# A hybrid decoder step on one core: the conv history, the last conv taps and y cross HBM with channels on the partitions

## What is computed

```python
def conv_ffn(h, hist, w_up, conv_w, conv_b, w_down):
    T = h.shape[1]
    g_pre, u = jnp.split(h @ w_up, 2, axis=-1)
    gp = jnp.concatenate([hist.astype(g_pre.dtype), g_pre], axis=1)
    conv = conv_b + conv_w[0] * gp[:, 0:T]
    for i in range(1, CONV_W):
        conv = conv + conv_w[i] * gp[:, i:i + T]
    y = (jax.nn.silu(conv) * u) @ w_down
    return y, gp[:, T:]
...
    x = x + gate2 * y
```

## Time and profile before

| | |
|---|---|
| median of 3 runs | 1593.41 us (1593.29 to 1593.66) |
| profiled execution, span from first to last instruction | 1592.4 us |
| PE busy | 1569.0 us (99%), 12242 matmuls |
| DVE, ACT, POOL busy | 899.9, 665.7, 74.4 us |
| mean granted TensorE clock | 0.995 |
| DMA | 371.06 MB, mean 233 GB/s |

### The profile page before, as it was taken

One profiled execution on the slowest core, in us unless ns is written; L12 is line 12 of the kernel. 1 busy time (PEld: TensorE's weight loads), 2 busy tenths in 40 slices (PEclk: granted clock), 3 DMA queues, 4 the chain that ended last, 5 costly groups with the idle time before them and its releaser, 6 DMA issues.

```text
span 1592.4 us, 29203 instructions
## 1 busy us (share of the span) xinstructions
PE 1569.0 (99%) x12242; PEld 1418.5 (89%) x12242; DVE 899.9 (57%) x1525; ACT 665.7 (42%) x935; POOL 74.4 (5%) x131
## 2 busy tenths in 40 slices
PE   8999999999999999999999999999999999999997
PEld 4777888888888658888899999999999999999997
DVE  3555776656667536447454545545454566656663
ACT  3433444434446335325333333333333445545552
POOL 2000000001111000000000000000000000000000
PEclk8999999999999999999999999999999999999999
DMA  9999877777778998988844444454545554555460
GB/s 338 387 366 329 303 263 265 254 269 242 243 261 297 390 398 300 330 321 302 284 159 161 161 161 160 160 185 142 181 164 171 166 162 147 191 157 191 146 192 20
DMA packets 239232, 371.06 MB, mean 233 GB/s; under 512 B 7793, under 2 KB 188371, under 8 KB 230905
## 3 DMA queue, kind: packets, MB, share of 16 engines
q1 hardware_dynamic: 231888, 351.19, 63.8%
q0 software_dynamic: 7152, 17.90, 3.4%
q10 hardware_dynamic: 66, 0.14, 0.0%
HBM read 359.32 MB, written 9.88 MB: 232 GB/s over the span
## 4 chain that ended last, share of the span: by engine, by line
PE 84%; DMA 5%; issue 5%; DVE 3%; SPq 2%; ACT 2%; POOL 0%; ACTq 0%; POOLq 0%; DVEq 0%
PE ps L1046 24%; PE ps L1047 23%; PE ps L1048 23%; PE ps L998 3%; PE ps L1289 2%; DMA ring<-in_w_in 2%; PE ps L991 1%; DMA proj<-in_cache_v_win 1%; DMA vals<-in_w_ada 1%; SPq L610 1%; DMA ring<-in_w_out 1%; DVE wlo L2173 1%; PE ps L1360 1%; PE ps L1329 1%; ACT whi L1608 1%
## 5 line engine op out<-in xcount | busy, mean ns | idle before, releaser
L1046 PE MATMUL ps<-hhi,whi 128*128 128x288 f32 x3120 | 929.7, 298 | 1.5 <-DVE wlo L2014 0.5
L1047 PE MATMUL ps<-hlo,whi 128*128 128x288 f32 x3120 | 917.1, 294 | 0.0
L1048 PE MATMUL ps<-hhi,wlo 128*128 128x288 f32 x3120 | 917.0, 294 | 0.0
L1046 PEld LDWEIGHTS ps<-hhi,whi 128*128 128x128 f32 x3120 | 585.3, 188 | 43.6 <-issue 33.9
L1047 PEld LDWEIGHTS ps<-hlo,whi 128*128 128x128 f32 x3120 | 585.6, 188 | 0.7
L1048 PEld LDWEIGHTS ps<-hhi,wlo 128*128 128x128 f32 x3120 | 585.4, 188 | 0.0
L2014 DVE TENSOR_TENSOR wlo<-ring,whi 128x1024 fp32r<-128x1024 f32 x178 | 212.2, 1222 | 89.2 <-ACT whi L1599 88.8
L1599 ACT ACTIVATE whi<-ring 128x1024 fp32r<-128x1024 f32 x178 | 184.2, 1056 | 155.0 <-PE ps L1048 148.4
L2173 DVE TENSOR_TENSOR wlo<-ring,whi 128x1024 fp32r<-128x1024 f32 x96 | 117.0, 1222 | 84.6 <-ACT whi L1608 84.4
L1608 ACT ACTIVATE whi<-ring 128x1024 fp32r<-128x1024 f32 x96 | 100.8, 1053 | 145.6 <-PE ps L1048 112.3
L2695 DVE TENSOR_TENSOR wlo<-ring,whi 128x1024 fp32r<-128x1024 f32 (+1 forms) x94 | 105.7, 1132 | 56.0 <-ACT whi L1935 56.0
(11 more groups left out here) (323 smaller groups left out, 1141.5 us busy)
## 6 DMA issues: line engine op xcount, KB each, us to landing
ring<-in_w_up SPq DMA_DIRECT2D x88, 1024.0 KB, 5.2
ring<-in_w_ada SPq DMA_DIRECT2D x64, 1024.0 KB, 7.6
ring<-in_w_in SPq DMA_DIRECT2D x48, 1024.0 KB, 8.1
ring<-in_w_down SPq DMA_DIRECT2D x32, 1408.0 KB, 6.7
proj<-in_w_ada SPq DMA_DIRECT2D x28, 1024.0 KB, 9.4
ring<-in_w_out SPq DMA_DIRECT2D x16, 1024.0 KB, 8.6
ring<-in_cache_k_win SPq DMA_DIRECT2D x12, 1024.0 KB, 8.5
proj<-in_cache_v_win SPq DMA_DIRECT2D x8, 1024.0 KB, 13.1
```

The costliest lines, as they stand in the source:

```text
L1046: mm(out, w_hi, x_hi, start=start, stop=False)
L1047: mm(out, w_hi, x_lo, start=False, stop=False)
L1048: return mm(out, w_lo, x_hi, start=False, stop=stop)
```

## The change

The host lays `state_conv` out as [partition, tile, 16 rows] ahead of the launch, and takes `new_conv` and `y` as [partition, tile, rows]; it rearranges them after. In the kernel:

- the whole history comes in one load of 128 x 704 elements into `tail`, at the point of the first load of before; DVE copies from it to `gpad`;
- DVE writes the last taps of all 44 tiles to `last_taps` (in `gates`), stored by one DMA behind the last turn;
- `yst` is stored as it is, two tiles at a time, by POOL;
- all turns of up and down on PE are gone, with ACT's and DVE's copies out of the banks, and the waits between them;
- the last chunk of down goes tile 2 first, then tile 3; DVE finishes tile 2 and tile 3 apart; ACT stores tile 2, SP stores tile 3;
- SP, not POOL, waits for the output DMAs.

```diff
@@ up and down, PE
-                pe.wait_ge(hist_in[par], i * 8 + (16 - 8 * par))
-                pe.wait_ge(*FV.upto("hist", i - 1))
-                pe.sem_inc(row_turns, 1)
-                for n in range(4):
-                    last = turn(ps[:, 4, 16 * n:16 * n + 16], hrow[:, par, P * n:P * n + P], ident[0:16, 0:16])
-                last.then_inc(*FT.step("hist"))
...
-                pe.wait_ge(*FV.upto("last", i))
-                pe.wait_ge(*FA.upto("rows", i - 1))
-                for n in range(4):
-                    last = turn(ps[0:18, 5, P * n:P * n + P], glast[:, n, :], ident)
-                last.then_inc(*FT.step("rows"))
...
-                            for k in range(nk):
-                                for n in range(2):
...
+                            end = i == 3 and j == 23
+                            order = [(k, n) for k in range(nk) for n in range(2)]
+                            for k, n in sorted(order, key=lambda kn: kn[1]) if end else order:
...
+                                if end and (k, n) == (nk - 1, 0):
+                                    last.then_inc(last_even_done, 1)
                             last.then_inc(used, 1)
-                            if i == 3 and j == 22:
-                                first_row_turns()
-                        if i and kg == 0 and h == 0:
...
-                            row_turns_of(i - 1)
-            row_turns_of(3)
@@ POOL
+            pool.dma_start(history.rearrange("p n b r -> p (n b r)"), a["state_conv"].rearrange("p n c -> p (n c)")
+                           ).then_inc(hist_in, 16)
+            pool.wait_ge(*FV.upto("last", 10))
+            pool.dma_start(o["new_conv"], last_taps).then_inc(conv_out, 16)
+            for i in range(4):
+                for h in range(2 if i < 3 else 1):
+                    pool.wait_ge(*DV_.upto(f"u{h}", i))
+                    pool.dma_start(o["y"][:, 4 * i + 2 * h:4 * i + 2 * h + 2], yst[:, 2 * h:2 * h + 2]
+                                   ).then_inc(y_out[h], 16)
@@ ACT
-                act.wait_ge(*FT.upto("rows", i))
-                act.wait_ge(conv_stored, i + 1)
-                f(crows, ps[0:18, 5, :], ACT.Copy).then_inc(*FA.step("rows"))
...
+            act.wait_ge(*DV_.upto("u1", 3))
+            act.dma_start(o["y"][:, 14], yst[:, 2]).then_inc(last_even_out, 16)
@@ DVE
-                dve.wait_ge(*FT.upto("hist", i))
+                dve.wait_ge(hist_in, 16)
                 v.tensor_copy(gpad[:, :, 2 + SEQ:GW].rearrange("p n (b t) -> p n b t", t=6)[:, :, :, 0:2],
-                              ps[:, 4, 0:64].rearrange("p (n b r) -> p n b r", n=4, b=NB)).then_inc(*FV.step("hist"))
+                              history[:, 4 * i:4 * i + 4]).then_inc(*FV.step("hist"))
...
-                    dve.wait_ge(*DT.upto("t2", i - 1))
+                    if i:
+                        dve.wait_ge(y_out[h], 16 * i)
...
+                def last_out():
+                    dve.wait_ge(y_out[1], 48)
+                    dve.wait_ge(last_even_done, 1)
+                    dve.wait_ge(*DV_.upto("u0", 3))
+                    gated(5 * KD, 14, ps[:, 2:3, :], lambda m: yst[:, 2, :], DV_, 1, 3)
+                    dve.wait_ge(used, 3 * 24 + (CH_DOWN + BUFS + 24))
+                    dve.wait_ge(*DV_.upto("u1", 3))
+                    gated(5 * KD, 15, ps[:, 3:4, :], lambda m: yst[:, 3, :], DE, 0, 0)
@@ SP
-            sp.wait_ge(first_row_out, 1)
-            sp.dma_start(o["y_p"][0:P, 1536:2048], yrow[0]).then_inc(y_end_out, 16)
+            sp.wait_ge(*DE.upto("u", 0))
+            sp.dma_start(o["y"][:, 15], yst[:, 3]).then_inc(last_odd_out, 16)
+            for s, n in ((conv_out, 16), (k_out, 256), (v_out, 256), (stp_out, 64), (s0_out, 128), (y_out[0], 64),
+                         (y_out[1], 48), (last_even_out, 16), (last_odd_out, 16)):
+                sp.wait_ge(s, n)
```

More of the change, by code:

```diff
@@ L903, in _ @@
[L903 to L915, removed]
@@ L1479, in up_turn @@
                     unit(2, 2 * n + 1, i * 16 + CH_UP, last_slabs(i, 2 * n + 1))
-                pe.wait_ge(*FV.upto("last", i))
-                pe.wait_ge(*FA.upto("rows", i - 1))
-                for n in range(4):
-                    last = turn(ps[0:18, 5, P * n:P * n + P], glast[:, n, :], ident)
-                last.then_inc(*FT.step("rows"))
-            for i in range(11):
[L1487 to L1511, removed]
+            for i in range(11):
+                up_turn(i)
             pe.wait_ge(*FA.upto("g1", 10))
@@ L2544, in _, with gated @@
             head_lo(1)
-            def gated(gate, tile, psum, out, steps, n, i, end=False):
-                tmp = tmp_s[:, 64 * (n % 2):64 * (n % 2) + 64]
-                ts = tmp.rearrange("p (n b t) -> p n b t", n=2, b=NB)
-                gs = modT[:, bass.ds(tile + gate, 2), 1:NC9].rearrange("p n (b a) -> p n b a", a=1)
+            def gated(gate, tile, psum, out, steps, n, i):
+                c = psum.shape[1]
+                tmp = tmp_s[:, 64 * (n % 2):64 * (n % 2) + NS * c]
+                ts = tmp.rearrange("p (n b t) -> p n b t", n=c, b=NB)
+                gs = modT[:, bass.ds(tile + gate, c), 1:NC9].rearrange("p n (b a) -> p n b a", a=1)
+                first, last_step = (f"s{n}", f"u{n}") if steps is not DE else ("s", "u")
                 v.tensor_tensor(ts, psum[:, :, SEQ:TOK].rearrange("p n (b t) -> p n b t", t=TS),
-                                gs.to_broadcast([P, 2, NB, TS]), ALU.mult).then_inc(*steps.step(f"s{n}"))
-                for m in range(2):
-                    last = v.scalar_tensor_tensor(
+                                gs.to_broadcast([P, c, NB, TS]), ALU.mult).then_inc(*steps.step(first))
+                for m in range(c):
+                    v.scalar_tensor_tensor(
                         out=out(m)[:, 0:SEQ], in0=psum[:, m, 0:SEQ],
@@ L2558, in gated @@
                         op0=ALU.mult, op1=ALU.add)
-                if end:
-                    last.then_inc(last_shown, 1)
-                dve.wait_ge(*steps.upto(f"s{n}", i))
-                for m in range(2):
+                dve.wait_ge(*steps.upto(first, i))
+                for m in range(c):
                     last = v.tensor_tensor(out(m)[:, SEQ:TOK], tmp[:, NS * m:NS * m + NS],
                                            xT[:, bass.ds(tile + m, 1), SEQ:TOK].rearrange("p a c -> p (a c)"), ALU.add)
-                last.then_inc(*steps.step(f"u{n}"))
+                last.then_inc(*steps.step(last_step))
             def out_tiles(n):
@@ L2696, in down_turn @@
                                     whi[:, jj % BUFS, 0:n].bitcast(F32), ALU.subtract).then_inc(lo_done, 1)
-                if end == 24:
+                if i < 3:
+                    out(1)
+                else:
                     out(0)
-                out(1, end == 24)
+                    last_out()
             dve.wait_ge(*FV.upto("act1", 10))
-            dve.wait_ge(*FT.upto("rows", 10))
             for i in range(4):
                 down_turn(i, 24 + LEAD if i < 3 else 24)
-            dve.wait_ge(*DT.upto("t1", 3))
-            dve.wait_ge(y_out, 144)
-            v.tensor_copy(yrow[1], ps[:, 5, :]).then_inc(second_row_out, 1)
 def qd_blocks(qd, h, lo):
```

109 lines of the change are left out of this document (35 added, 74 removed).

## The result

| | before | changed |
|---|---|---|
| median of the runs | 1593.41 us (1593.29 to 1593.66) | **1571.11 us** (1570.13 to 1571.87) |
| ratio, 95% interval | | 0.9861, 0.9847 to 0.9875 |
| profiled execution, its span | 1592.4 us | 1569.2 us |
| mean granted clock | 0.995 | 0.996 |
| PE busy, matmuls | 1569.0 us, 12242 | 1552.1 us, 12106 |

The forecast was 1572.2 us with 1570.2 to 1575.2, and a span of 1571.2 us: the median came out 1.1 us lower, the span 2.0 us lower. The forecast took 1.0 us from the span to the time, from one median and one profile. Of the later runs each has its own span on record: before lies 1.57 us above it (43 runs, 1.51 to 1.63), the changed kernel 1.85 (8 runs, 1.58 to 1.97). Their median spans are 1591.5 and 1569.4 us, 22.1 us apart, so the first profile of before (1592.4) is a long one.

The account below looks back on a forecast made before the run. PE, 99% busy, was taken to bound the kernel, its feeders following. Turns 15.0 plus end 6.9 less history load 0.7 make 21.2 us, so 1593.4 becomes 1572.2 us, range 1570.2 to 1575.2.

Parts of the forecast that it names:

- The turns: PE in up and down: removing the turns from the matmul stream gains 15.0 us, bounds 14.3 to 15.4.
- up's 1.00 us for a border: PE between two turns of up: the eight small turns there cost 1.00 us, at 10 places, 10.0 us.
- the cover: Up's turn 0, 719.28 us: PE's 0.5 us wait for DVE's lower weights hides four turns' 0.4 us, so no gain.
- a turn is worth its duration: Rival, PE in up and down: each turn removed gives its single written 0.27 us, 34.0 us, so 1553.2 us; chance 1%.
- The feeders: Rival at a turn's first chunk: PE waits for ACT or DVE instead, the 15.0 us stay, 1587.2 us; chance 3%.
- The end: Behind PE's last product: span ends at 1585.5 instead of 1592.4 us, gaining 6.9 us, bounds 5.9 to 7.5.
- the end stays: Rival at the program's end: POOL's DRAIN is not over in time, giving back up to 6.9 us, 1579.1 us; chance 5%.
- The history load: DMA-full stage, 540 to 580 us: 295 KB more push cached values and PE back, costing 0.7 us, bounds 0 to 1.5.
- The last rival: PE's wait at 572 us reaches 2.2 us or more, the clock falls: 1593.5 us or more; chance 1%.
- The rival of the whole landing: Cached values wait for the history load's whole 5.9 us landing on POOL's queue: 5.2 us more, 1577.4 us; chance 6%.
- the sum on record: Whole kernel: predicted total gain of 21.2 us, from 15.0 + 6.9 - 0.7.

## Why the prediction was right

**The turns: right.** 14.8 us against 15.0. The term that was a little too large is up's 1.00 us for a border; it measured 0.98 at nine borders and 0.88 at the first. Turn 0's turns gave nothing, as said, but the cover is another one than the prediction named. The wait for the lower part of the weights lies 12 us further on, at 733 us in before, and is 0.4 to 0.5 us in both kernels. What takes the turns' place is a wait of 0.42 us at up's first product, at 719.74 us, for the lower part of the activations from DVE (`hlo`), which before doesn't have. The turns put back cost 10.0 us for 80, 0.12 us each, so the rival "a turn is worth its duration" is out by experiment, not only by the sum; the page "TensorE: Matmul & The Clock Gate" of the Trainium skill, section "Part 4: PE-mode transpose", gives a duration, some 275 ns in one kernel's context. The trace agrees with it (0.27 us for one turn). That section states no price in a stream, and the 0.12 us are what these runs show for it.

**The feeders: right.** PE has no idle time from 820 to 1560 us, and what the later products are ahead by grows at the turns' places and nowhere else.

**The end: right in its sum, with small errors in its terms.** 7.3 us against 6.9; the terms as listed add up to 1585.6 us, not 1585.5, so to 6.8. I gave SP's DRAIN 0.135 us, from the row where it stood behind an issue; behind the waits it took 7 ns. I took 2.2 us for the landing, which was 1.86. POOL's DRAIN began with its issue and lasted 3.2 us instead of 4.4, which changes nothing, as it was out of the way by either. By the profiles the 7.3 us are made of:

| part | us | from |
|---|---|---|
| the waits on SP instead of POOL | 2.3 | before with that edit alone (2.2 by median spans) |
| the last store issued 0.74 us behind PE, POOL's was 2.8 | 2.05 | both timelines |
| landing 1.86 us, POOL's of 256 KB was 2.8 | 0.9 | both timelines |
| POOL's DRAIN begun 7 us ahead of PE's end | 2.1 | the rest |

The rival "the end stays" needed POOL's DRAIN to last over 11 us from its new start; it took 3.2.

Not all of it reaches the metric. A run's time lies 1.57 us above its span in before, 1.60 with the waits back on POOL in the changed kernel, 1.72 in before with the waits on SP, and 1.85 in the changed kernel. So ending the program on SP gives back some 0.15 to 0.25 us outside the span, which the prediction had as a constant of 1.0 us. What fills this time isn't in a trace.

**The history load: within its bounds of 0 to 1.5 us, but its loss of 0.7 us isn't seen.** Moving the 360 KB away gains 0.6 us, where their bytes give 0.9, so the step that bytes in this stage push PE back holds. But the term was the difference to before, and there PE's wait didn't grow from 1.5 to 2.2 us: it is 1.2 to 2.1 us in the six profiles with the load in place and 1.3 to 1.9 in the three of before's code there. By these waits the two loads of 32 KB cost about as much as the one of 360 KB; no run has before without them, so why stays open. Beyond one load there is a second part that the working lacked: one more load costs 2.0 us and three more 5.5, with a clock that falls for 3.4 us in both profiles. The last rival had this chain, a clock that falls behind PE's wait at 572 us, but put its point at a wait of 2.2 us and four such stretches for its price; the fall came as a single one of 1.7 us, behind 1.9 to 3.9 us of waits. The rival of the whole landing, 5.2 us more, falls: a load that took 6.8 us to land cost 0.6. (Its 5.9 us were the landing of a store of y; a load of history took 4.9.)

**Why 1.1 us lower than forecast.** In medians before and after differ by 22.3 us, and by 21.9 from the repeat of before to the eight runs of after; the sum on record was 21.2. The spans of the later runs differ by 22.1 us, which is what turns and end give, 14.8 + 7.3, and nothing is left for the history load, either way. Against the sum on record the turns gave 0.2 us less, the end 0.4 more, the history load took 0.7 less, and 0.3 came on outside the span: 21.8. The rest, up to 0.5 us, is of the size by which two profiles of the same code differ ahead of 580 us. The forecast is right by its large terms, and most of its error is the history load's.

## What to carry to other kernels

Price an operation in a full matmul stream by the distance between its neighbours' starts, less the normal step, and put it back alone to prove it: here 0.12 us, where 0.27 was written. At the end of a program look at who waits for the last store and whose DRAIN follows: an engine that issues its last DMA early and then has nothing to wait for takes its DRAIN off the path. Price a changed load against what stood at its place before, not against nothing. And a new load belongs outside the stage in which the bounding engine already waits for DMA, even when it costs only half a microsecond there, since in the runs with more of it the clock fell as well.

## What the runs showed of the hardware beyond what was expected

- The clock fell for 3.4 us in three profiles (before with SP's waits, the load twice, the load four times), after PE had waited 1.9, 2.0 and 3.9 us for cached values near 570 us. It stayed at 1.00 with waits of 0.7 to 1.8 us in the others, and also with 2.1 us in the kernel with the last tiles together. So around 2 us it may or may not fall, and the wait alone doesn't decide it. No single wait in the three profiles was over 1.6 us.
- POOL's DRAIN has no fixed length: 4.4 us in both profiles of before, 5.0 when it began together with the last issue there (4.4 from that issue's end), 3.2 in both of the changed kernel, 2.9 behind a last store of one tile, 1.6 behind a wait for all of them. Every case of before is longer than every case of the changed kernel. What sets it wasn't found.
- SP's DRAIN took 135 ns behind an issue and 7 ns behind waits.
- POOL's stores of y landed in 2.7 us, where they took 5.9 us, with 288 KB instead of 256; DMA's share in the stage is the same, the layout in HBM isn't. No run separates the two layouts alone.
